# Sliding attention's projections in tiles, with the normalisation and rotation chains placed between them

## The reference, cut to what matters

```python
def qkv_heads(a, w_qkv, q_norm, k_norm, n_heads, n_kv, hd):
    b, s, _ = a.shape
    q, k, v = jnp.split(a @ w_qkv, [n_heads * hd, (n_heads + n_kv) * hd], axis=-1)
    q = rms_norm(split_heads(q, n_heads, hd), q_norm).reshape(b, n_kv, n_heads // n_kv, s, hd)
    k = rms_norm(split_heads(k, n_kv, hd), k_norm)
    v = split_heads(v, n_kv, hd)
    return q, k, v
...
    q, k, v = qkv_heads(a_lat, w_qkv, q_norm, k_norm, WIN_HEADS, WIN_KV, WIN_HD)
    qc, kc, vc = qkv_heads(a_ctx, w_qkv, q_norm, k_norm, WIN_HEADS, WIN_KV, WIN_HD)
    q = apply_rope(q, cos, sin)
    k = apply_rope(k, cos, sin)
```

## Time and profile before

| | |
|---|---|
| median of 3 runs | 2245.79 us (2243.2 to 2246.06) |
| the profiled execution's own time | 2239.34 us |
| its span | 2237.5 us |
| busy PE / DVE / ACT | 2052.2 / 855.6 / 379.1 us |
| mean granted TensorE clock | 0.957 |

### The profile page before, as it was taken

One profiled execution on the slowest core, in us unless ns is written; L12 is line 12 of the kernel. 1 busy time (PEld: TensorE's weight loads), 2 busy tenths in 40 slices (PEclk: granted clock), 3 DMA queues, 4 the chain that ended last, 5 costly groups with the idle time before them and its releaser, 6 DMA issues.

```text
span 2237.5 us, 40982 instructions
## 1 busy us (share of the span) xinstructions
PE 2052.2 (92%) x18732; PEld 1763.0 (79%) x18732; DVE 855.6 (38%) x1431; ACT 379.1 (17%) x693; POOL 14.9 (1%) x10
## 2 busy tenths in 40 slices
PE   7989889999998989889999999858899999999999
PEld 4778578799997778578899997524688888878878
DVE  4767683200005748553200003266466501113320
ACT  3021412000002022411000003124211101012110
POOL 0000000000000000000000000000000000000000
PEclk8999989999999999989999999979999999999999
DMA  9991564399993662453599993200288734434420
GB/s 360 387 340 62 183 226 191 123 367 384 397 395 144 223 223 94 151 184 122 187 360 383 401 388 113 81 0 0 75 286 281 271 123 149 151 113 151 143 102 19
DMA packets 184179, 466.03 MB, mean 208 GB/s; under 512 B 5153, under 2 KB 55681, under 8 KB 176385
## 3 DMA queue, kind: packets, MB, share of 16 engines
q1 hardware_dynamic: 183776, 463.83, 56.5%
q10 hardware_dynamic: 288, 0.52, 0.1%
HBM read 463.29 MB, written 1.05 MB: 208 GB/s over the span
## 4 chain that ended last, share of the span: by engine, by line
PE 81%; DVE 12%; ACT 3%; issue 3%; DMA 1%; SPq 0%; DVEq 0%; ACTq 0%
PE pair L359 80%; DVE AR L1472 1%; DMA ring<-in_ada_w 1%; DVE SM L2004 1%; DVE AR L1975 1%; ACT AR L1357 1%; ACT AR L1196 1%; DVE AR L1689 1%; DVE RST L1527 1%; DVE AR L2002 0%; DVE XH L1472 0%; DVE AR L2003 0%; DVE AR L1699 0%; SPq L250 0%; PE pair L860 0%
## 5 line engine op out<-in xcount | busy, mean ns | idle before, releaser
L359 PE MATMUL pair<-XH,ring 128*128 128x256 f32 (+4 forms) x3584 | 816.5, 390 | 21.4 <-ACT XH L1099 17.3
L359 PE MATMUL pair<-AR,ring 128*64 128x96 f32 (+1 forms) x12992 | 808.5, 262 | 29.3 <-issue 15.2
L359 PEld LDWEIGHTS pair<-AR,ring 128*64 128x64 f32 (+1 forms) x12992 | 761.0, 143 | 75.0 <-issue 22.1
L359 PEld LDWEIGHTS pair<-XH,ring 128*128 128x128 f32 (+3 forms) x3584 | 684.3, 192 | 137.5 <-issue 28.3
L1942 DVE TENSOR_TENSOR AR<-AR,pair 128x384 f32<-128x384 f32 x30 | 16.6, 554 | 449.9 <-PE pair L359 449.9
L1472 DVE SCALAR_TENSOR_TENSOR AR<-ring,CACT,AR 128x512 f32<-128x512 f32 x245 | 184.2, 752 | 8.7
L359 PE MATMUL pair<-AR 128*128 128x128 f32 (+6 forms) x640 | 139.9, 385 | 20.0 <-ACT AR L1370 15.5
L359 PEld LDWEIGHTS pair<-AR 128*128 128x128 f32 (+3 forms) x640 | 90.9, 183 | 61.6 <-ACT AR L1370 28.1
L1559 DVE SCALAR_TENSOR_TENSOR XH<-pair,MOD,XH 128x256 f32<-128x256 f32 x64 | 28.3, 480 | 214.6 <-PE pair L359 214.5
L2036 DVE SCALAR_TENSOR_TENSOR AR<-pair,VEC,AR 128x255 f32<-128x255 f32 x88 | 41.9, 476 | 114.6 <-ACT AR L1395 114.6
L1301 ACT ACTIVATE AR<-pair 128x768 f32 x30 | 24.5, 815 | 306.1 <-PE pair L359 306.1
(11 more groups left out here) (248 smaller groups left out, 1124.8 us busy)
## 6 DMA issues: line engine op xcount, KB each, us to landing
ring<-in_ada_w SPq DMA_DIRECT2D x48, 2048.0 KB, 12.7
ring<-in_w_gate SPq DMA_DIRECT2D x32, 2048.0 KB, 9.1
ring<-in_w_up SPq DMA_DIRECT2D x32, 2048.0 KB, 9.4
ring<-in_w_down SPq DMA_DIRECT2D x32, 2048.0 KB, 9.5
ring<-in_ffn_w_up SPq DMA_DIRECT2D x44, 1024.0 KB, 7.6
ring<-in_w_in SPq DMA_DIRECT2D x18, 2048.0 KB, 12.1
ring<-in_ffn_w_down SPq DMA_DIRECT2D x8, 2048.0 KB, 8.5
ring<-in_sc_w_in SPq DMA_DIRECT2D x6, 2048.0 KB, 7.9
```

The source lines that it names most:

```text
L359: return pe.matmul(o, lhsT, rhs, start=start, stop=stop, **kw)
```

## The change

PE's order of the projections is now query half 0, keys, query half 1, values, and the chains' matmuls stand between tiles of the later projections. The chains run in the order query half 0 (i = 0), keys (i = 1), query half 1 (i = 2). Each chain's sums and rotation matmuls overwrite the PSUM tile from which its part was copied (`QP`), where they used a tile of another part before; squares and roots lie in other blocks of `AR`. Doubling the keys stands ahead of the second query half's rotation, and the copy of the values is ACT's last step, behind the copies of the doubled keys. DVE takes one chain after the other, where it had the next part's norm ahead of each rope. A semaphore `wk_made` is new. The core of the diff:

```diff
-            for k, q in enumerate((PA, PB)):
-                done(features(ck("wqkv", k), [half(q, m) for m in range(4)], lambda t: H2[:, t, 0:S],
-                              first=5 if k == 0 else None))
+            QT, QP = [blk(0), blk(4), blk(1)], [PA, PC, PB]
...
+            def wsums(i):
+                pe.wait_ge(s["wsq_ready"], i + 1)
+                for m in range(2):
+                    last = mm(QP[i][:, 512 * m:512 * m + 512], cB, blk(2 + i % 2)[:, 512 * m:512 * m + 512], True, True)
+                last.then_inc(s["wsum_ready"], 1)
+
+            def wrotated(i):
+                pe.wait_ge(s["wn_ready"], i + 1)
+                n = S if i == 1 else 512
+                for m in range(2):
+                    last = mm(QP[i][:, n * m:n * m + n], cP, QT[i][:, 512 * m:512 * m + n], True, True)
+                last.then_inc(s["wrot_ready"], 1)
...
+            wk_tile(0)
             wsums(0)
...
+            wk_tile(1).then_inc(s["wk_made"], 1)
+            arrived(ck("wqkv", 1))
+            wq_tile(ck("wqkv", 1), PB, 0)
+            wsums(1)
+            wq_tile(ck("wqkv", 1), PB, 1)
+            wrotated(0)
+            wq_tile(ck("wqkv", 1), PB, 2)
+            done(wq_tile(ck("wqkv", 1), PB, 3))
+            wv_tile(0)
+            wsums(2)
+            wrotated(1)
+            wv_tile(1)
+            wv_tile(2)
+            pe.wait_ge(s["wroped"], 2)
             for g in range(4):
...
             last.then_inc(s["k_dup"], 1)
+            wrotated(2)
+            done(wv_tile(3))
+            pe.wait_ge(s["wroped"], 3)
...
-            for u in range(3):
-                multiplied(ck("wqkv", u))
-                A(QT[u], (PA, PB, PC)[u], ACT.Copy).then_inc(s["wq_copied"], 1)
-            A(blk(7), PD, ACT.Copy).then_inc(s["wv_copied"], 1)
...
+            for i in range(3):
+                if i == 1:
+                    act.wait_ge(s["wk_made"], 1)
+                else:
+                    multiplied(ck("wqkv", i // 2))
+                A(QT[i], QP[i], ACT.Copy).then_inc(s["wq_copied"], 1)
+                act.wait_ge(s["wq_copied"], i + 1)
+                A(blk(2 + i % 2), QT[i], ACT.Square).then_inc(s["wsq_ready"], 1)
+                act.wait_ge(s["wsum_ready"], i + 1)
+                if i == 2:
+                    act.wait_ge(s["wn_ready"], 1)
+                A(blk(10 + i % 2), QP[i], ACT.Sqrt, scale=1.0 / WHD, bias=EPSC[:, 0:1]).then_inc(s["wstd_ready"], 1)
             act.wait_ge(s["k_dup"], 1)
             A(blk(5), PA, ACT.Copy)
             A(blk(6), PC, ACT.Copy).then_inc(s["kdup_copied"], 1)
+            multiplied(ck("wqkv", 2))
+            A(blk(7), PD, ACT.Copy).then_inc(s["wv_copied"], 1)
...
+            for i in range(3):
+                gcol, std = (V_WQ, V_WK, V_WQ)[i], blk(10 + i % 2)
+                V.wait_ge(s["wstd_ready"], i + 1)
                 link(V.reciprocal(std, std))
-                V.scalar_tensor_tensor(QT[u], QT[u], VEC[:, gcol:gcol + 1], std, ALU.mult, ALU.mult).then_inc(s["wn_ready"], 1)
...
+                V.scalar_tensor_tensor(QT[i], QT[i], VEC[:, gcol:gcol + 1], std, ALU.mult, ALU.mult).then_inc(s["wn_ready"], 1)
+                V.wait_ge(s["wrot_ready"], i + 1)
```

More of the change, by code:

```diff
@@ L231, in stack_program @@
         hp_turned hp_ready xe_ready ys_copied yt_turned yt_act yt_dve scattered
-        wq_copied wsum_ready wstd_ready wn_ready wrot_ready wroped k_dup kdup_copied wv_copied
+        wk_made wq_copied wsum_ready wstd_ready wn_ready wrot_ready wroped k_dup kdup_copied wv_copied
         wsq_ready ot_ready ot_copied
@@ L896, in _, with wq_tile, wk_tile, wv_tile @@
             h2k = lambda t: H2[:, t, :]
-            for k, q in enumerate((PA, PB)):
-                done(features(ck("wqkv", k), [half(q, m) for m in range(4)], lambda t: H2[:, t, 0:S],
-                              first=5 if k == 0 else None))
+            QT, QP = [blk(0), blk(4), blk(1)], [PA, PC, PB]
+            def wq_tile(c, q, m, first=None):
+                w = view(c, KT, 512)
+                for t in range(KT):
+                    if first is not None:
+                        h_tile(first, t)
+                    last = mm(half(q, m), w[:, t, m * P:m * P + P], H2[:, t, 0:S], t == 0, t == KT - 1)
+                return last
+            def wk_tile(m):
+                w = view(ck("wqkv", 2), KT, 512)
+                for t in range(KT):
+                    last = mm(PC[:, 512 * m:512 * m + 512], w[:, t, m * P:m * P + P], H2[:, t, :], t == 0, t == KT - 1)
+                return last
+            def wv_tile(m):
+                w = view(ck("wqkv", 2), KT, 512)
+                for t in range(KT):
+                    last = mm(PD[:, S * m:S * m + S], H2[:, t, m * P:m * P + P], w[:, t, 256:512], t == 0, t == KT - 1)
+                return last
+            def wsums(i):
[9 more added lines that the diff above has]
+                last.then_inc(s["wrot_ready"], 1)
+            arrived(ck("wqkv", 0))
+            for m in range(4):
+                last = wq_tile(ck("wqkv", 0), PA, m, 5 if m == 0 else None)
+            done(last)
             arrived(ck("wqkv", 2))
@@ L903, in _ @@
                 h_tile(5, t, 1)
[L904 to L922, removed]
-            wsums(0)
-            for u in range(3):
[L926 to L936, removed]
+            wk_tile(0)
+            wsums(0)
+            wk_tile(1).then_inc(s["wk_made"], 1)
[12 more added lines that the diff above has]
+            pe.wait_ge(s["wroped"], 2)
             for g in range(4):
@@ L939, in _ @@
                 o = (PA, PC)[g // 2][:, 512 * (g % 2):512 * (g % 2) + 512]
-                last = mm(o, sel, QT[2][:, 512 * (g // 2):512 * (g // 2) + 512], True, True)
+                last = mm(o, sel, QT[1][:, 512 * (g // 2):512 * (g // 2) + 512], True, True)
             last.then_inc(s["k_dup"], 1)
+            wrotated(2)
+            done(wv_tile(3))
+            pe.wait_ge(s["wroped"], 3)
             KDUP = AR[:, 5 * 1024:7 * 1024].rearrange("p (g n) -> p g n", g=4)
@@ L1327, in _ @@
             shifted(5, H2[:, :, S:2 * S], 1, 0, 0, 1)
-            QT = [blk(0), blk(1), blk(4)]
-            for u in range(3):
-                multiplied(ck("wqkv", u))
-                A(QT[u], (PA, PB, PC)[u], ACT.Copy).then_inc(s["wq_copied"], 1)
-            A(blk(7), PD, ACT.Copy).then_inc(s["wv_copied"], 1)
[L1335 to L1348, removed]
+            QT, QP = [blk(0), blk(4), blk(1)], [PA, PC, PB]
+            for i in range(3):
[10 more added lines that the diff above has]
+                A(blk(10 + i % 2), QP[i], ACT.Sqrt, scale=1.0 / WHD, bias=EPSC[:, 0:1]).then_inc(s["wstd_ready"], 1)
             act.wait_ge(s["k_dup"], 1)
```

18 lines of the change are left out of this document (4 added, 14 removed).

## The result

The changed kernel took 2207.76 us, the median of four runs (2204.76 to 2211.16), against 2245.93 before: a ratio of 0.9833 with a 95% interval of 0.9815 to 0.9851. It is faster, by 38 us in this comparison. The forecast was 2213.8 us, with a range of 2209.5 to 2220, so the direction and most of the amount were right, but the time lies 1.7 us under the range. Over all executions made in this study (85 of the kernel before, 14 of the changed one) the means are 2243.9 and 2208.9 us, which is 35.0 us or a ratio of 0.9844. Single executions of one and the same kernel scatter with a standard deviation of 3.7 us (before) and 2.7 us (changed), so this difference is known to about 1.6 us either way. Taken comparison by comparison, the three differences of means are 37.5, 33.3 and 35.4 us.

A forecast was written before the change was run, and what follows sets the result against it. PE, busy 92% of the span, was taken as the bound. Its 55.2 us of work plus ACT's copy put first scores at 1448.8 instead of 1480.39, 31.6 us saved, taken as 32: 2245.79 - 32 = 2213.8 us, range 2209.5 to 2220.

The forecast's parts named there:

- PE's sum: From query half 0's end: projections 41.35, sums 5.55, rotations 4.63, doubling 3.70, together 55.2 us if PE never waits.
- the groups of four records: Sums and rotations inside PE's stream: priced at 1.85 us; if cheaper, six groups give up to 0.9 us more.
- 8 foreseen: Ahead of its first rope, DVE waits 8 us for the rotation placed behind tile 1 of query half 1.
- the last one: Last norm, ahead of query half 1's rotation: ends at 1441.7, PE arrives at 1442.3, 0.6 us to spare.
- The copy of the values was the last step: At the stage's end, ACT's 1.02 us values copy ends at 1448.8, after the last rope, and the first scores start.
- given back: Rival in the feed-forward part: a transfer or another chain loses up to 32 us again; chance 0.02.
- the late chain: Rival at the keys' and last rotations: DVE's lateness adds 3 to 8 us, saving 24 to 29; chance 0.10.
- the flickering clock: Rival in the stage: short waits bring PE's clock to 0.93, 55.2 us become 59.4, 27.8 saved; chance 0.04.
- My first rival: DVE's chain is late and PE pays at the keys' and last rotations, 2217 to 2222 us; chance 0.10.
- the last one of the sum: Whole kernel: the runs' median lies 6.5 us above the profiled execution, so 2245.79 - 32 gives 2213.8 us.
- more than that: Rival: inserted groups nearly free and later stages gain a little, 34 to 38 us saved, 2208 to 2212; chance 0.04.

The follow-up runs named there:

- the last value tile taken out: Changed kernel with value tile 3 behind the first two scores and its copy behind the first softmax; stage 54.48 us, mean 2207.2 us, ratio 0.9835 to the kernel before.
- the one with the other semaphore numbers: Kernel before with only the additional semaphore declared, unused, so later semaphores have other numbers; mean 2243.6 us, ratio 0.9999.
- DVE's chain early, with PE's last waits filled: Changed kernel with earlier rotations, value tile 1 ahead of the last rotation; value tile 2 behind or ahead of first scores: 2205.0 or 2205.5 us.

## Why the prediction was right and where it was wrong

**The stage: right.** What bounds it, what moves and what follows came as written. PE's sum was 55.2 us, and the row has 54.2 of busy PE; scores were worked out at 56.35 us behind query half 0 (1448.8 - 1392.45), with up to 0.9 less if the groups of four records cost less in a stream. They do: a group adds 1.72 us (1403.96 to 1405.68) where I took 1.85, and the stage took 55.43. DVE waited 8.1 us for the first rotation (8 foreseen). The keys' norm ended at 1434.48, 0.5 us ahead of PE, as foreseen; the last one 0.35 us ahead, for which I had 0.6. The copy of the values was the last step, the rope 0.85 us ahead of it. That this balance is real and not a figure of speech is shown by the kernels around it: one tile later at the first rotation costs 4.8 us, and the last value tile taken out gains 0.95.

**What follows: right.** The rest from the first scores to the end is 755.96 to 757.8 us in the three profiles of the changed kernel and 757.1 to 758.8 in the four of before (the one with the other semaphore numbers among them); nothing was given back. Of the rivals, the late chain and the flickering clock did not occur (clock 1.00 over the stage in all three profiles), and the interleaved groups had no wait ahead of them. What sets the first of them off can now be said: with a rotation one tile (3.45 us) later, PE waited 2.9 us and lost 1.7 more to the clock behind the wait. My first rival's price, a lateness paid one to one, was therefore too low in that profile. It is not a fixed price: the same waits of 2.97 and 3.71 us were followed by the lower clock in some profiles and by 1.00 in others.

**The step that failed** is the last one of the sum: "The median of the runs lies 6.5 above that execution, so I predict 2245.79 - 32", with the range around it. The miss of 6.0 us has three parts, and only one is in the sum:

- 1.9 us: the three runs shown were high for this kernel. Their median is 2245.79; the mean of 85 executions is 2243.9.
- 1.1 us: the four first runs of the changed kernel were low. Their median is 2207.76, the mean of 14 is 2208.9.
- 3.0 us: the change saves 35.0 us and not 32. Of this, 0.5 us are the groups above. Some 0.6 us are the stage of before, which was 87.94 us in the profile that I read and 88.5 on average. The other 1.9 us are not settled. The difference of the means is known to about 1.6 us and the average stage of before, from four profiles that spread over 3 us, to about 1.4, so it may be scatter. But 1 to 3 us of this kind remain in each of the eight kernels that have the changed order on ACT and DVE, which would fit a stage of before that is longer on average than 88.5; no run here shows it. The rest averages 756.8 us for the changed kernel and 757.8 for that of before, with ranges that overlap; neither the start of the projections nor half 0 separates the two, and an effect of the semaphores' numbers was not seen.

I had used the scatter of the three runs (2.9 us) as if it bounded a median. One execution scatters by 3.7 us, the median of three or four by some 2, and a difference of two such medians by about 3. From 2243.9 the same sum gives 2211.9, still 4.1 us over the measured median; with such scatter a range of 2206 to 2220 would have been the honest one. The case "more than that", 34 to 38 us, got a chance of 0.04 because I looked for a mechanism for it and not at the noise of what I subtracted from.

**How it gets better.** DVE's chain early, with PE's last waits filled (none over 1.4 us is left), brings the stage to 52.6 us and the mean to 2205. PE then waits 0.26 us for the last rope ahead of the scores, so DVE's chain and PE's sum are again within 1 us of each other.

## What to carry to other kernels

Two stages that each leave the other's engine idle gain much of the shorter one if they are interleaved by tiles (here 32.5 of 41.3 us, since the chains hold work of PE too), and the sum of one engine's records between two fixed points is then a good forecast: here it was right to 1 us in 55. Work out the arrival of both engines at each join, because a wait can cost more than its length: behind waits of 2.2 to 3.7 us PE ran at the lower clock for a while in some profiles and not in others. Filling one with an independent tile is worth what the next limit allows: here 2.3 us in the stage for a wait of 2.87, since DVE's last rope then came last, and 0.4 for one of 2.23. And compare sums with means over many executions; three runs don't fix the point from which one subtracts.

## What was unexpected in the hardware

- The clock fell after the wait, not in it, in the kernel with the first rotation late: PE stood 2.87 us, worked at 1.00 for 1.4 us, and then ran at 0.50 for about 3.4 us while it was busy. The Trainium skill, in "TensorE: Matmul & The Clock Gate", section "HAM oscillation — how this bites in real kernels", describes bursts of matmuls that begin at the lower clock after each wait for data. This trace agrees in that the lower clock came behind a wait; that the fall can come 1.4 us into the next burst is this trace's.
- The same wait does not always bring the fall. Behind 2.97 us ahead of the first sums the clock was 1.00 in three profiles of the kernel before, and the matmuls took 3.70 us; in the fourth they took 6.71. Behind 3.71 us ahead of the first scores these took 1.99, 2.45, 3.69 and 3.79 us in four kernels. What decides it is open.
- The time of the same code ahead of the projections differed by up to 12.5 us between profiled executions (projections start at 1372.3 to 1384.8 us). Among the four profiles of the kernel before, which lie up to 11.8 us apart, nearly all of it is PE's busy time, at a lower mean clock; what decides the clock in one execution stays open.
- The kernel with the first rotation late had a rest of 759.8 us, 1 to 4 us more than all others. In it the clock stood at the lower level for some 54 us, against 34 to 50 in the other thirteen profiles, which would account for part of it; why it did is not shown, and there is one profile.
